# Second block's gate and value tiles 3 to 20 as seven half-depth, half-token block products for eight, with the weight sums on GpSimd and the gated tiles rounded later

## The chip, the cores and the metric

The kernel runs on one core of a Trainium2 chip. The metric is the device time of one execution in microseconds (us); lower is better. The core has a matrix engine, TensorE (PE in the rows; its weight loads are PEld), and three engines for elementwise work: VectorE (DVE), ScalarE (ACT) and GpSimd (POOL). SyncE (SP) issues the transfers from HBM. Each engine has a program of its own and goes through it in order; they are ordered among each other by semaphores only. Matmul results land in PSUM, everything else on the chip lies in SBUF. Both have 128 partitions.

## The reference

Two model blocks run one after the other on 512 tokens of width 1024, in float32. The change concerns the second block, which has two layers, and in it only the gated feed-forward network:

```python
def rmsnorm(x, g, eps=NORM_EPS):
    xf = x.astype(jnp.float32)
    y = xf * lax.rsqrt(jnp.mean(xf * xf, axis=-1, keepdims=True) + eps)
    return y.astype(x.dtype) * g

def swiglu(h, w_gate, w_up, w_down):
    return (jax.nn.silu(h @ w_gate) * (h @ w_up)) @ w_down

def second_block(x, ...):
    for l in range(DEPTH):
        x = x + 0.5 * swiglu(rmsnorm(x, ffn1_norm[l]), ffn1_w_gate[l], ffn1_w_up[l], ffn1_w_down[l])
        h = rmsnorm(x, mix_norm[l])
        ...
        x = x + 0.5 * swiglu(rmsnorm(x, ffn2_norm[l]), ffn2_w_gate[l], ffn2_w_up[l], ffn2_w_down[l])
    return rmsnorm(x, final_norm)
```

There are two layers (DEPTH is 2); the dots in the loop stand for three token mixers, whose output is added to x. The hidden width is 2752, 21 tiles of 128 and one of 64. So the feed-forward network runs four times; each run is called a part below.

## The kernel before

**Layout.** Activations lie with the feature on the partition and the 512 tokens along the row. A weight tile is 128 x 128, and a *unit* is a piece of weights that comes in one transfer: eight such tiles side by side, 128 x 1024 (all eight depth steps k of one gate or value tile), or 128 x 896 for seven tiles of the down projection. A part has 43 units of gate and value (gate tile 0, value tile 0, gate tile 1, ...; the last holds the 64 columns of both) and then 24 of the down projection, three for each of eight output tiles.

**Precision.** A float32 product is made of three matmuls of a reduced type (fp32r in the rows): each operand is split into a rounded part `hi` and a remainder `lo`, and the sum is hi x hi + hi x lo + lo x hi. So a unit of eight tiles is 24 matmuls of 512 columns, and a gate and value tile is 48. The split of a unit is ScalarE's rounding (`Stream.split_hi`, L682) and VectorE's subtraction of 1024 columns (`Stream.split_lo`, L690). SyncE loads units into four raw buffers (`one_raw`), the split ones lie in three places (`two_w_hi`, `two_w_lo`), and `Stream.multiply` (L705) waits for the split and signals `unit_done`, on which the rounding of the unit three further on waits.

**A part.** The RMS norm's gain goes onto x first (ScalarE L597, `two_x_hi`; the remainder VectorE L602); the norm's factor for each token (`m.rstd`, made while the first units are multiplied) is multiplied onto the results. For each tile t, VectorE scales the gate product out of PSUM into one of two `mid` rows (L1482), ScalarE applies Silu to it in place (L1258), VectorE multiplies it with the value product from PSUM (L1488, the gated product) and scales again (L1491), ScalarE rounds the result to `two_h_hi` (L1262), and VectorE makes the remainder `two_h_lo` (L1496). Splits of the units to come stand between these steps, at places written out by hand: one ahead of the gated product, one ahead of the remainder.

```python
for t in range(FT2):
...
    st.split_lo(dve, u + min(2 * t + 5, IN2 + 3))
...
    st.split_lo(dve, u + min(2 * t + 6, IN2 + 4))
...
```

TensorE uses PSUM banks 2 (t mod 3) and the next for tile t. After the 22 tiles comes the down projection with 128 x 512 hidden tiles as the moving operand: each of the eight output tiles takes three units, of eight, seven and seven hidden tiles (its three thirds). In the very last part the last output tile is made in two token halves of 256 columns (`last_tile`, L1085).

**Parts and stages.** The four parts lie in three stages (`chain_stage`); the first part starts directly behind the last norm of the first block (its first three gate and value tiles run beside the end of that norm), the other three behind the output projection of a mixer or behind the part before. GpSimd has nothing to do in them.

## Time and profile before

| what | value |
|---|---|
| time, median of 3 runs | 3702.64 us (3702.22 to 3707.24) |
| profiled execution, span from first to last instruction | 3696.9 us |
| TensorE busy | 3586.1 us, 97% |
| VectorE busy | 2026.3 us, 55% |
| ScalarE busy | 1432.0 us, 39% |
| GpSimd busy | 139.1 us, 4% |
| DMA | 82 GB/s on average |
| mean granted TensorE clock | 0.984 of full speed |
| part starts (first scaling, L1482) | 1476.7, 2223.6, 2576.3, 3346.2 us |

A busy share is the time in which an engine had an instruction under way, over the span. The profile lists no time of its own for the profiled execution beside its span; the median of the runs lies 5.7 us above that span. A row of the timeline gives the start, the duration, the engine, the line of the program, the operation, and the operands with their shapes and types; what stands in brackets is how long the engine had been idle before it and which work ended that wait.

### The profile page before, as it was taken

To read this page: it belongs to the slowest core of one execution; us is meant where nothing else is said; L and a number is where in the kernel's file an instruction comes from. 1 tells how busy PE (TensorE), PEld (TensorE's weight loads), DVE (VectorE), ACT (ScalarE), POOL (GpSimd) and SP (SyncE) were. 2 spreads that over 40 slices of the span, in tenths; PEclk is the share of its full clock that TensorE was granted. 3 is DMA by queue.
4 is the path that set the end of the run, shared out by engine and by line. 5 is a ranking of instruction groups with operands and counts; after the bars stand their busy time and mean duration, and the time that the engine had idled before them with its cause. 6 is when DMAs were issued, how large, how long until landed. Compare 5 with 4: busy or idle time off the path is not lost. (4 is left out here: it accounts for less than half of the span.)

```text
span 3696.9 us, 61545 instructions
## 1 busy us (share of the span) xinstructions
PE 3586.1 (97%) x26295; PEld 3100.4 (84%) x26295; DVE 2026.3 (55%) x3385; ACT 1432.0 (39%) x2297; POOL 139.1 (4%) x189
## 2 busy tenths in 40 slices
PE   8999999899999998999999999999999999999999
PEld 8999999788899998888877678888888877668887
DVE  7667653544476635543478564444444478565443
ACT  6844332544453324332243343223222244343232
POOL 0000000011000000000003100000000002100000
PEclk9999999999999998999999999999999999999999
DMA  3232223122212232333320023333333320013332
GB/s 136 80 98 84 91 91 92 64 76 76 69 64 92 91 94 76 99 96 98 111 69 3 24 80 97 97 94 101 97 97 94 110 80 2 24 64 99 97 95 80
DMA packets 87872, 303.21 MB, mean 82 GB/s; under 512 B 9632, under 2 KB 11808, under 8 KB 87344
## 3 DMA queue, kind: packets, MB, share of 16 engines
q1 hardware_dynamic: 87600, 299.28, 25.7%
q8 instruction: 208, 3.41, 0.4%
q14 instruction: 64, 0.52, 0.0%
HBM read 297.11 MB, written 2.13 MB: 81 GB/s over the span
## 5 line engine op out<-in xcount | busy, mean ns | idle before, releaser
L690 DVE TENSOR_TENSOR two_w_lo<-one_raw,two_w_hi 128x1024 fp32r<-128x1024 f32 (+1 forms) x334 | 400.5, 1199 | 754.7 <-ACT two_w_hi L682 752.6
L705 PE MATMUL psum<-two_x_hi,two_w_hi 128*128 128x512 f32 x1768 | 694.6, 393 | 1.2 <-DVE two_rows L1488 0.9
L705 PE MATMUL psum<-two_x_hi,two_w_lo 128*128 128x512 f32 x1768 | 688.4, 389 | 0.0
L705 PE MATMUL psum<-two_x_lo,two_w_hi 128*128 128x512 f32 x1768 | 687.9, 389 | 0.0
L682 ACT CAST two_w_hi<-one_raw 128x1024 fp32r<-128x1024 f32 (+1 forms) x334 | 342.0, 1025 | 823.6 <-PE psum L705 817.1
L705 PEld LDWEIGHTS psum<-two_x_hi,two_w_hi 128*128 128x128 f32 x1768 | 331.8, 188 | 88.8 <-issue 17.8
L2286 PE MATMUL psum<-one_x_hi,one_w_hi 128*128 128x264 f32 (+1 forms) x1376 | 391.6, 285 | 7.8 <-DVE one_x_lo L790 7.3
L705 PEld LDWEIGHTS psum<-two_x_hi,two_w_lo 128*128 128x128 f32 x1768 | 331.8, 188 | 69.8
L705 PEld LDWEIGHTS psum<-two_x_lo,two_w_hi 128*128 128x128 f32 x1768 | 331.9, 188 | 69.4 <-issue 1.4
L2286 PE MATMUL psum<-one_x_lo,one_w_hi 128*128 128x264 f32 (+1 forms) x1376 | 389.4, 283 | 0.0
L2286 PE MATMUL psum<-one_x_hi,one_w_lo 128*128 128x264 f32 (+1 forms) x1376 | 389.0, 283 | 0.0
L705 PE MATMUL psum<-two_h_hi,two_w_hi 128*128 128x512 f32 x794 | 308.9, 389 | 0.0
L705 PE MATMUL psum<-two_h_hi,two_w_lo 128*128 128x512 f32 x794 | 308.9, 389 | 0.0
L705 PE MATMUL psum<-two_h_lo,two_w_hi 128*128 128x512 f32 x763 | 296.8, 389 | 0.0
L2286 PEld LDWEIGHTS psum<-one_x_hi,one_w_hi 128*128 128x128 f32 x1376 | 259.4, 189 | 10.3 <-DVE one_x_lo L790 9.6
L2286 PEld LDWEIGHTS psum<-one_x_lo,one_w_hi 128*128 128x128 f32 x1376 | 259.8, 189 | 0.0
L2286 PEld LDWEIGHTS psum<-one_x_hi,one_w_lo 128*128 128x128 f32 x1376 | 259.5, 189 | 0.0
L690 DVE TENSOR_TENSOR one_w_lo<-one_raw,one_w_hi 128x1024 fp32r<-128x1024 f32 (+2 forms) x145 | 170.6, 1179 | 124.8 <-ACT one_w_hi L682 123.0
L2286 PE MATMUL psum<-one_h_hi,one_w_hi 128*128 128x264 f32 (+1 forms) x704 | 198.9, 283 | 2.4 <-ACT one_pads L2391 2.4
L2286 PE MATMUL psum<-one_h_lo,one_w_hi 128*128 128x264 f32 (+1 forms) x704 | 199.0, 283 | 0.0
L2286 PE MATMUL psum<-one_h_hi,one_w_lo 128*128 128x264 f32 (+1 forms) x704 | 198.6, 282 | 0.0
L682 ACT CAST one_w_hi<-one_raw 128x1024 fp32r<-128x1024 f32 (+2 forms) x145 | 146.8, 1015 | 112.4 <-PE psum L2286 108.5
(540 smaller groups left out, 6723.1 us busy)
## 6 DMA issues: line engine op xcount, KB each, us to landing
one_raw<-in_swi_in SPq DMA_DIRECT2D x172, 512.0 KB, 3.5
one_raw<-in_ffn_in SPq DMA_DIRECT2D x88, 512.0 KB, 3.6
one_raw<-in_swi_out SPq DMA_DIRECT2D x64, 448.0 KB, 3.2
one_raw<-in_mix_in SPq DMA_DIRECT2D x54, 512.0 KB, 3.5
one_raw<-in_attn_w SPq DMA_DIRECT2D x32, 512.0 KB, 3.8
one_raw<-in_swi_out SPq DMA_DIRECT2D x32, 512.0 KB, 3.5
one_raw<-in_ffn_out SPq DMA_DIRECT2D x32, 448.0 KB, 3.3
one_raw<-in_lru_w SPq DMA_DIRECT2D x24, 512.0 KB, 5.3
```

What stands on the lines that cost most here:

```text
L682: self.nc.scalar.copy(self.place(u)[0], self.m.raw[:, u % self.RAW, 0:self.cols(u)]).then_inc(self.s["w_hi"], 1)
L690: self.nc.vector.tensor_tensor(lo, self.m.raw[:, u % self.RAW, 0:self.cols(u)], hi.bitcast(FP32), ALU.subtract).then_inc(self.s["w_lo"], 1)
L705: last = self.nc.tensor.matmul(self.m.ps[:, bank, :], a[:, w], b[:, k0 + k, :], start=(start and k == 0 and q == 0), stop=(stop and k == n ...
L2286: ins = nc.tensor.matmul(m.ps[:, bank + h, skip:HALF], a[:, w], b[:, k0 + k, h * HALF + skip:(h + 1) * HALF], start=(start and q == 0), st ...
```

## The change

**The products.** Tile t of gate and value, for t from 3 to 20, is one 2 x 2 block product: the weights are cut by gate and value and by the upper and lower four of the eight depth steps, the inputs by depth in the same way and by the first and last 256 tokens. That takes eight block products; the changed kernel makes seven, of sums of blocks (Winograd's form of Strassen's method). Each product is four depth steps of three matmuls with 256 columns. The products share their partial results through PSUM: ScalarE copies three partial sums of 256 columns out of it for each tile (`take`), and VectorE adds them to other products (`join`). The other tiles (0 to 2 and the one of 64) and the down projection keep their form.

**The sums.** For each tile GpSimd makes three sums of 128 x 512 of the raw weights for the next tile (`sum_weights`) and one for this one (`sum_last`), and at the part's start four of 128 x 1024 of the inputs (`sum_inputs`), from copies of x that ScalarE scales with the gain (`gain`, eight). The splits of a tile are now A and B (1024 columns), C, D and E (512): A and E come from the raw weights, B, C and D from the sums. A raw buffer is free again when the splits and the sums have read it.

**The hidden tiles.** The memory of the sums of inputs (`mixed`, `mixed_raw`) is that of the hidden tiles from 6 on. So the gated tiles are kept raw in `h_raw` (in the place of `two_h_lo`), and only tiles 0 to 5 are rounded as they come; the rounding and the remainders of tiles 6 to 20 come at the part's end.

```diff
+class Seven:
+    FIRST, LAST, NOW = 3, 20, 6
+    HALF, DEEP = SEQ // 2, KT // 2
...
+        self.done = self.count("done", [x for t in steps for x in (
+            now(t, 1, 2) + now(t - 1, 3, 4) + now(t, 6, 7, 5))])
...
+    def multiply(self, pe, t, p, bank, start, stop):
+        name = {1: "A", 2: "A", 6: "B", 5: "B", 7: "C", 3: "D", 4: "E"}[p]
+        pe.wait_ge(self.s["c_lo"], self.splits[t, name])
+        hi, lo = self.place(p)
+        for k in range(self.DEEP):
+            w, (x_hi, x_lo) = slice(k * P, (k + 1) * P), self.block(p, k)
+            for q, (a, b) in enumerate(((hi, x_hi), (hi, x_lo), (lo, x_hi))):
+                last = self.nc.tensor.matmul(self.m.ps[:, bank, 0:self.HALF], a[:, w], b, start=(start and k == 0 and q == 0),
+                                             stop=(stop and k == self.DEEP - 1 and q == 2), skip_group_check=True)
+        last.then_inc(self.s["c_done"], 1)
...
+    def first_products(self, pe, t):
+        self.emptied(pe, t, "A")
+        self.multiply(pe, t, 1, self.bank(t, "A"), True, False)
+        self.emptied(pe, t, "B")
+        self.multiply(pe, t, 2, self.bank(t, "B"), True, True)
...
+    def sum_inputs(self, pool):
+        pool.wait_ge(self.s["taken"], self.takes["x", KT - 1])
...
+            self.nc.gpsimd.tensor_tensor(raw(i, 1), left, right, ALU.subtract).then_inc(self.s["w_sum"], 1)
+
+    def sum_weights(self, pool, t):
...
+        self.nc.gpsimd.tensor_tensor(w[1], self.raw(t, 1, 0), self.raw(t, 1, 1), ALU.add).then_inc(self.s["w_sum"], 1)
+        if t > self.FIRST:
+            pool.wait_ge(self.s["c_lo"], self.splits[t - 1, "D"])
+        pool.wait_ge(self.s["w_sum"], self.sums[t, 1])
+        self.nc.gpsimd.tensor_tensor(w[0], w[1], self.raw(t, 0, 0), ALU.subtract).then_inc(self.s["w_sum"], 1)
+        self.nc.gpsimd.tensor_tensor(w[2], self.raw(t, 0, 0), self.raw(t, 1, 0), ALU.subtract).then_inc(self.s["w_sum"], 1)
+
+    def sum_last(self, pool, t):
+        w = self.m.w_sums[:, 0, :]
+        pool.wait_ge(self.s["c_lo"], self.splits[t, "B"])
+        self.nc.gpsimd.tensor_tensor(w, self.raw(t, 0, 1), w, ALU.subtract).then_inc(self.s["w_sum"], 1)
...
+                    for t in seven.tiles:
+                        seven.first_products(pe, t)
+                        if t > seven.FIRST:
+                            seven.last_products(pe, t - 1)
+                        seven.middle_products(pe, t)
+                    pe.wait_ge(s["scaled"], part.h + seven.LAST)
+                    st.multiply(pe, part.u + 2 * REST, 2 * (REST % 3), m.xs, 0, True, True)
+                    seven.last_products(pe, seven.LAST)
```

TensorE makes products 1 and 2 of a tile first, then 3 and 4 of the tile before, then 6, 7 and 5.

**VectorE inside the tiles.** Before, one tile's rows are these (the letters after the line are the operation, then output and inputs by the names in SBUF, and the shape); a psum among the inputs is a read from PSUM:

```order
L1482 TENSOR_TENSOR two_rows<-psum,two_rows 128x512
L690 TENSOR_TENSOR two_w_lo<-one_raw,two_w_hi 128x1024
L1488 TENSOR_TENSOR two_rows<-psum,two_rows 128x512
L1491 TENSOR_TENSOR two_rows<-two_rows 128x512
L690 TENSOR_TENSOR two_w_lo<-one_raw,two_w_hi 128x1024
L1496 TENSOR_TENSOR two_h_lo<-two_rows,two_h_hi 128x512
```

In the changed program a tile from 8 on has these. L1000 is a split (by their order B, C, A of the next tile, D, E), L1018 a join, L1024 and L1028 the scalings of the gate's two token halves, L1035 the gated product, L1816 the scaling behind it:

```order
L1000 TENSOR_TENSOR two_w_lo<-two_w_sums,two_w_hi 128x1024
L1000 TENSOR_TENSOR two_w_lo<-two_w_sums,two_w_hi 128x512
L1018 TENSOR_TENSOR two_rows<-psum,two_rows 128x256
L1024 TENSOR_TENSOR two_rows<-two_rows 128x256
L1000 TENSOR_TENSOR two_w_lo<-one_raw,two_w_hi 128x1024
L1028 TENSOR_TENSOR two_rows<-psum,two_rows 128x256
L1000 TENSOR_TENSOR two_extra_lo<-two_w_sums,two_extra_hi 128x512
L1018 TENSOR_TENSOR two_h_raw<-psum,two_rows 128x256
L1035 TENSOR_TENSOR two_rows<-two_h_raw,two_rows 128x512
L1816 TENSOR_TENSOR two_h_raw<-two_rows 128x512
L1000 TENSOR_TENSOR two_w_lo<-one_raw,two_w_hi 128x512
L1018 TENSOR_TENSOR two_h_raw<-psum,two_rows 128x256
```

Six rows become twelve, the hidden tile's remainder has left, and the gated product reads both operands from SBUF.

**GpSimd.** Before, it has no row in a part. Now a part begins with the four sums of inputs, and then each tile has four sums of weights:

```order
L1044 TENSOR_TENSOR two_mixed_raw<-two_mixed_raw 128x1024 x4
L1050 TENSOR_TENSOR two_w_sums<-one_raw 128x512
L1054 TENSOR_TENSOR two_w_sums<-two_w_sums,one_raw 128x512
L1055 TENSOR_TENSOR two_w_sums<-one_raw 128x512
L1060 TENSOR_TENSOR two_w_sums<-one_raw,two_w_sums 128x512
```

All of these are new; the last one of a tile waits for VectorE's split B, the second for the split D of the tile before.

**The start of a part, ScalarE and VectorE.** On ScalarE, the rows behind the square root of the norm (L626) are before:

```order
L626 ACTIVATE two_rows<-psum,eps 128x512
L1258 ACT_TABLE_LOAD
L1258 ACTIVATE two_rows<-two_rows 128x512
L1262 CAST two_h_hi<-two_rows 128x512
L1258 ACTIVATE two_rows<-two_rows 128x512
L682 CAST two_w_hi<-one_raw 128x1024
```

In the first part they now are (L969 the copies of x, L1511 Silu, L1517 the rounding of a hidden tile, L975 the roundings of the sums of inputs, L995 those of the weights):

```order
L626 ACTIVATE two_rows<-psum,eps 128x512
L969 ACTIVATE two_mixed_raw<-x_tokens,vectors 128x2x256 x8
L1511 ACT_TABLE_LOAD
L1511 ACTIVATE two_rows<-two_rows 128x512
L1517 CAST two_h_hi<-two_h_raw 128x512
L975 CAST two_mixed<-two_mixed_raw 128x1024 x2
L1511 ACTIVATE two_rows<-two_rows 128x512
L975 CAST two_mixed<-two_mixed_raw 128x1024 x2
L1517 CAST two_h_hi<-two_h_raw 128x512
L995 CAST two_w_hi<-one_raw 128x1024
```

And VectorE, from the first scaling (L1801) to the split A of tile 3 (the first L1000), with the remainders of the sums of inputs in L980:

```order
L1801 TENSOR_TENSOR two_rows<-psum,two_rows 128x512
L1810 TENSOR_TENSOR two_rows<-psum,two_rows 128x512
L1816 TENSOR_TENSOR two_h_raw<-two_rows 128x512
L1822 TENSOR_TENSOR two_h_lo<-two_h_raw,two_h_hi 128x512
L1801 TENSOR_TENSOR two_rows<-psum,two_rows 128x512
L980 TENSOR_TENSOR two_mixed<-two_mixed_raw,two_mixed 128x1024 x2
L1810 TENSOR_TENSOR two_rows<-psum,two_rows 128x512
L1816 TENSOR_TENSOR two_h_raw<-two_rows 128x512
L1822 TENSOR_TENSOR two_h_lo<-two_h_raw,two_h_hi 128x512
L980 TENSOR_TENSOR two_mixed<-two_mixed_raw,two_mixed 128x1024 x2
L1801 TENSOR_TENSOR two_rows<-psum,two_rows 128x512
L1000 TENSOR_TENSOR two_w_lo<-one_raw,two_w_hi 128x1024
```

The eight copies stand between the norm's root and the first Silu; the four remainders of 1024 columns stand ahead of split A, for which product 1 of tile 3 waits. In the other parts the splits of units 4 to 6 (L703) stand between these rows as well.

**The end of a part, VectorE.** Behind the join of product 7 of tile 20 and the split of the down projection's first unit, VectorE has these rows up to the split (L703) for the down projection's second third. L1822 is the remainder of a hidden tile (x2: two of them), and the shapes with 64 are the last, narrow tile:

```order
L1822 TENSOR_TENSOR two_h_lo<-two_h_raw,two_h_hi 128x512 x2
L1028 TENSOR_TENSOR two_rows<-psum,two_rows 128x256
L1801 TENSOR_TENSOR two_rows<-psum,two_rows 64x512
L1822 TENSOR_TENSOR two_h_lo<-two_h_raw,two_h_hi 128x512 x2
L1018 TENSOR_TENSOR two_h_raw<-psum,two_rows 128x256
L1035 TENSOR_TENSOR two_rows<-two_h_raw,two_rows 128x512
L1816 TENSOR_TENSOR two_h_raw<-two_rows 128x512
L1822 TENSOR_TENSOR two_h_lo<-two_h_raw,two_h_hi 128x512 x2
L1810 TENSOR_TENSOR two_rows<-psum,two_rows 64x512
L1816 TENSOR_TENSOR two_rows<-two_rows 64x512
L1822 TENSOR_TENSOR two_h_lo<-two_h_raw,two_h_hi 128x512 x2
L703 TENSOR_TENSOR two_w_lo<-one_raw,two_w_hi 128x896
```

Before, each remainder stood inside its tile, and nothing but a split and the remainder of the last tile stood between the last scaling and the down projection.

## Rows read from the trace of the kernel before

**Rows 1.** The page, part 1: busy time, share of the span, instructions.

```profile
PE 3586.1 (97%) x26295; PEld 3100.4 (84%) x26295; DVE 2026.3 (55%) x3385; ACT 1432.0 (39%) x2297; POOL 139.1 (4%) x189
```

**Rows 2.** Windows, inside a part: length, busy PE, PEld, DVE, ACT, POOL, PEclk, DMA, GB/s.

```profile
1520.00:1640.00 120.00, 120.00 (x531) 99.34 (x531) 54.72 (x68) 35.73 (x44) 0.00 (x0) 1.00 0.31 97
```

**Rows 3.** Timeline of VectorE inside the gate and value tiles.

```profile
1568.08 1.23 DVE L690 TENSOR_TENSOR two_w_lo<-one_raw,two_w_hi 128x1024 fp32r<-128x1024 f32 x1 [3.01 <-ACT two_w_hi L682]
1569.22 0.68 DVE L1488 TENSOR_TENSOR two_rows<-psum,two_rows 128x512 f32<-128x512 f32 x1
1569.94 0.69 DVE L1491 TENSOR_TENSOR two_rows<-two_rows 128x512 f32<-128x512 f32 x1
1573.52 1.23 DVE L690 TENSOR_TENSOR two_w_lo<-one_raw,two_w_hi 128x1024 fp32r<-128x1024 f32 x1 [2.89 <-ACT two_w_hi L682]
1574.66 0.69 DVE L1496 TENSOR_TENSOR two_h_lo<-two_rows,two_h_hi 128x512 fp32r<-128x512 f32 x1
1575.26 0.69 DVE L1482 TENSOR_TENSOR two_rows<-psum,two_rows 128x512 f32<-128x512 f32 x1
1578.96 1.23 DVE L690 TENSOR_TENSOR two_w_lo<-one_raw,two_w_hi 128x1024 fp32r<-128x1024 f32 x1 [3.01 <-ACT two_w_hi L682]
```

**Rows 4.** The chain that ended last, in order of time: start, length, what.

```profile
3338.31 332.34 PE psum L705 x1466
3670.65 13.19 PE psum L1085 x110
```

**Rows 5.** Lines by form, VectorE, from the second block's token mixers.

```profile
L3539 DVE TENSOR_TENSOR two_ring<-psum,two_ring 128x256 f32<-128x256 f32 x8 | 3.2, 420 | 1.6 <-PE psum L3327 1.6
```

**Rows 6.** Lines by form, ScalarE: the gain onto x, and the Silu table.

```profile
L597 ACT ACTIVATE two_x_hi<-x_tokens,vectors 128x512 fp32r<-128x512 f32 x40 | 29.0, 725 | 152.7 <-DVE x_tokens L1404 152.7
...
L1258 ACT ACT_TABLE_LOAD x4 | 5.1, 1283 | 0.1
```

**Rows 7.** Lines by form, GpSimd, from the second block's token mixers.

```profile
L3517 POOL TENSOR_TENSOR two_y<-two_ring 128x512 f32<-128x512 f32 x6 | 7.6, 1268 | 0.5
L2685 POOL TENSOR_TENSOR two_low<-two_low,two_high 128x768 f32<-128x768 f32 x4 | 7.2, 1813 | 0.0
```

**Rows 8.** Timelines of GpSimd and VectorE in the first block's attention.

```profile
712.27 0.30 POOL L1867 COPY one_convs<-one_bias 128x128 f32<-128x128 f32 x1
712.31 1.32 DVE L2012 TENSOR_TENSOR one_w_lo<-one_raw,one_w_hi 128x1024 fp32r<-128x1024 f32 x1
...
719.06 1.33 DVE L2012 TENSOR_TENSOR one_w_lo<-one_raw,one_w_hi 128x1024 fp32r<-128x1024 f32 x1
719.26 1.19 POOL L1855 COPY one_convs<-one_bias 128x16 f32<-128x16 f32 x1
720.41 1.28 POOL L1856 TENSOR_TENSOR one_convs<-one_bias,causal 128x512 f32<-128x512 f32 x1
720.51 1.75 DVE L2055 TENSOR_SCALAR one_logits<-one_logits,stat 128x400 f32<-128x400 f32 x2
721.84 0.42 DVE L2055 TENSOR_SCALAR one_logits<-one_logits,stat 128x400 f32<-128x400 f32 x1
721.93 1.45 POOL L1856 TENSOR_TENSOR one_convs<-one_bias,causal 128x512 f32<-128x512 f32 x1
```

**Rows 9.** The page, part 6: issues of a unit's transfer, median from issue to landing.

```profile
one_raw<-in_swi_in SPq DMA_DIRECT2D x172, 512.0 KB, 3.5
```

**Rows 10.** Lines by form: the down projection's splits and matmuls.

```profile
L690 DVE TENSOR_TENSOR two_w_lo<-one_raw,two_w_hi 128x896 fp32r<-128x896 f32 x64 | 69.9, 1093 | 124.1 <-ACT two_w_hi L682 124.1
L705 PE MATMUL psum<-two_h_hi,two_w_hi 128*128 128x512 f32 x794 | 308.9, 389 | 0.0
```

**Rows 11.** Timelines at the starts of the third part and the first.

```profile
2562.59 0.39 PE L705 MATMUL psum<-two_x_hi,two_w_hi 128*128 128x512 f32 x1
2573.96 1.05 ACT L682 CAST two_w_hi<-one_raw 128x1024 fp32r<-128x1024 f32 x1 [4.85 <-PE psum L705]
2596.40 1.05 ACT L682 CAST two_w_hi<-one_raw 128x1024 fp32r<-128x1024 f32 x1 [1.27 <-PE psum L705]
...
1472.63 0.69 ACT L626 ACTIVATE two_rows<-psum,eps 128x512 f32<-128x512 f32 x1 [2.46 <-PE psum L621]
1478.94 0.50 PE L705 MATMUL psum<-two_x_hi,two_w_hi 128*128 128x512 f32 x1 [0.86 <-DVE two_rows L1488]
```

**Rows 12.** Timeline and window of TensorE behind a wait in the first block.

```profile
163.50 0.36 PE L268 MATMUL psum<-one_hid_hi,one_lru_mix_hi 128*128 128x264 f32 x1 [2.94 <-ACT one_lru_cross L356]
164.50:168.00 3.50, 3.50 (x18) 0.51 0.40 109
```

More of the change, by code:

```diff
@@ L1121, in _ @@
                         first_units(part, rms, (0, 1))
-                    for t in range(3 if carried and part.first else 1, FT2):
-                        if t >= 3:
-                            pe.wait_ge(s["product"], part.h + t - 2)
-                        for g in range(2 if t < REST else 1):
+                    seven = sevens[part]
+                    for t in range(3 if carried and part.first else 1, seven.FIRST):
+                        for g in range(2):
                             st.multiply(pe, part.u + 2 * t + g, 2 * (t % 3) + g, m.xs, 0, True, True)
+                    for t in seven.tiles:
[6 more added lines that the diff above has]
+                    seven.last_products(pe, seven.LAST)
                     pe.wait_ge(s["std_ready"], part.p + 1)
@@ L1253, in _, with open_gate @@
                 if part.kind == "ffn":
-                    st.split_hi(act, u + 4)
-                    for t in range(FT2):
+                    seven = sevens[part]
+                    def open_gate(t):
                         act.wait_ge(s["scaled"], part.h + t + 1)
@@ new lines, in _ @@
+                    seven.take(act, seven.LAST, "u4")
+                    st.split_hi(act, u + IN2 + 1)
+                    act.wait_ge(s["c_done"], seven.done[seven.LAST, 5])
+                    for t in range(seven.NOW, seven.NOW + 4):
+                        round_hidden(t)
+                    open_gate(seven.LAST)
+                    for t in range(seven.NOW + 4, seven.NOW + 6):
+                        round_hidden(t)
+                    open_gate(REST)
+                    for t in range(seven.NOW + 6, seven.NOW + 8):
+                        round_hidden(t)
@@ L1263, in _ @@
+                    st.split_hi(act, u + IN2 + 2)
+                    act.wait_ge(s["c_done"], seven.done[seven.LAST, 4])
+                    for t in range(seven.NOW + 8, seven.LAST - 2):
+                        round_hidden(t)
+                    st.split_hi(act, u + IN2 + 3)
+                    for t in range(seven.LAST - 2, FT2):
+                        round_hidden(t)
+                    st.split_hi(act, u + IN2 + 4)
                     u += IN2
@@ new lines, in _ @@
+                    for t in seven.tiles:
+                        if t > seven.FIRST:
+                            seven.join(dve, t - 1, "C22")
+                            seven.split_lo(dve, t, "B")
+                        seven.split_lo(dve, t, "C")
+                        dve.wait_ge(s["hidden"], part.h + t - 1)
+                        seven.join(dve, t, "C11")
+                        seven.scale_first(dve, t)
+                        if t < seven.LAST:
+                            seven.split_lo(dve, t + 1, "A")
+                        else:
+                            st.split_lo(dve, u + IN2)
+                        if t > seven.FIRST:
+                            seven.scale_last(dve, t - 1)
+                        seven.split_lo(dve, t, "D")
+                        if t > seven.FIRST:
+                            seven.join(dve, t - 1, "C21")
+                            seven.gated(dve, t - 1)
+                            to_hidden(t - 1)
+                        seven.split_lo(dve, t, "E")
+                        if t - 1 < seven.NOW:
+                            rest_of_hidden(t - 1)
@@ new lines, in _ @@
+                    seven.join(dve, seven.LAST, "C22")
+                    st.split_lo(dve, u + IN2 + 1)
+                    for t in range(seven.NOW, seven.NOW + 2):
+                        rest_of_hidden(t)
+                    seven.scale_last(dve, seven.LAST)
+                    scale(REST)
+                    rest_of_hidden(seven.NOW + 2)
+                    rest_of_hidden(seven.NOW + 3)
+                    seven.join(dve, seven.LAST, "C21")
+                    seven.gated(dve, seven.LAST)
@@ new lines, in _ @@
+                    to_hidden(seven.LAST)
+                    for t in range(seven.NOW + 4, seven.NOW + 6):
+                        rest_of_hidden(t)
+                    gated(REST)
+                    to_hidden(REST)
+                    for t in range(seven.NOW + 6, seven.NOW + 8):
+                        rest_of_hidden(t)
+                    st.split_lo(dve, u + IN2 + 2)
+                    for t in range(seven.NOW + 8, seven.LAST - 2):
+                        rest_of_hidden(t)
+                    st.split_lo(dve, u + IN2 + 3)
@@ L1498, in _ @@
+                    for t in range(seven.LAST - 2, FT2):
+                        rest_of_hidden(t)
+                    st.split_lo(dve, u + IN2 + 4)
                     u += IN2
```

320 lines of the change are left out of this document (278 added, 42 removed).

## The prediction, made before the changed kernel had run

> **What bounds the kernel now.** I read the page's busy line first: TensorE is busy for 97% of a span of 3696.9 us, VectorE for 55%, ScalarE for 39%, GpSimd for 4% [rows 1]. Then the busy time by window: in a stretch inside the gate and value tiles TensorE is busy all of the time, VectorE 46%, GpSimd not at all [rows 2]. The VectorE timeline gives the length of a tile there: a weight split stands at 1568.08 and the same one of the next tile at 1578.96, so a tile takes 10.88 us [rows 3]. It holds 48 matmuls of 512 columns; the chain of waits has 1466 of these in 332.34 us, 226.7 ns each, and 48 x 226.7 is 10.88 again [rows 4]. So these tiles are bound by TensorE alone, and what takes away matmul time there shortens the span as long as the engines that feed it keep up. The durations are those of the profiled execution, whose span lies 5.7 us under the median of 3702.64. I take these 5.7 us as lying around the span and unchanged: the profiled execution then stands for 3702.6, which to the tenth is the median of the runs, and the sum below goes from there.
>
> **What the change removes from TensorE.** Tiles 3 to 20 are 18 tiles in each of four parts, 72 in all. A tile becomes 7 products of 4 x 3 matmuls of 256 columns, 84. The rows have that very shape in the last output tile: 110 matmuls in 13.19 us, 119.9 ns [rows 4]. 84 x 119.9 is 10.07 us, not 7/8 of 10.88 (9.52), because a half-length matmul costs more than half. The gain is 0.81 us a tile, **-58.3 us** over 72, if nothing else waits.
>
> **What it puts on VectorE.** One tile's queue, by the rows of order above: two splits of 1024 columns (A, B), three of 512 (C, D, E), three joins, one first and one last scaling of 256, the gated product and its scaling of 512. A 1024 split lasts 1.23 us and the next instruction starts 0.09 before it ends, so it takes 1.14 of the queue; one of 512 lasts 0.68 to 0.69 and takes 0.60 [rows 3]. For 256 columns the nearest row is 0.42 [rows 5], 0.34 of the queue. Two (the first join, the gated product) have a successor that needs their result; I count these full. Sum: 2 x 1.14 + 4 x 0.60 + 4 x 0.34 + 0.42 + 0.69 = 7.15, say 7.2 us. That alone would fit in 10.07. ScalarE fits too: two copies of 1024 (1.05 each, [rows 11]) and seven shorter steps of at most 0.73 [rows 6] are 7.2.
>
> **What it puts on GpSimd, and whom that stops.** Four sums of 512 columns a tile; such a row takes 1.27 us [rows 7]. The rows show that GpSimd and VectorE stop each other. At 719.26 a GpSimd copy of 16 columns takes 1.19 us: it ends 0.06 after a VectorE subtraction with two SBUF inputs (719.06 to 720.39). The other way, a subtraction of the split's own shape begins at 712.31, with a GpSimd copy running to 712.57, and takes 1.32 in place of 1.23. Two scalings from 720.51, alongside GpSimd's sum (720.41 to 721.69), take 1.75 together, though the second, from 721.84, takes 0.42: the first ended at about 721.92, 0.23 after the sum. And the sum from 721.93 takes 1.45, to 1.12 after that second scaling [rows 8]. So whoever comes second waits for the whole of the other and then needs its streaming time only: about 0.54 us for 512 VectorE columns, 1.07 for 1024 (712.57 to 713.63), 1.11 for a GpSimd sum. Instructions with one operand in PSUM I take as not stopped; [rows 5] is one, some of them beside GpSimd's work. Of VectorE's twelve, eight have two SBUF inputs.
>
> The Trainium skill, SBUF — State Buffer, on the shared port pair, states the same exclusion, for VectorE with two SBUF inputs against a GpSimd instruction that reads SBUF, and says that it is held for the whole instruction. By that last point the eight instructions and the four sums would stand end to end, 11.4 us a tile; by the rows the loser's start-up overlaps the wait, and the tile is the 10.4 laid out next.
>
> I lay one tile out with B at 0. B ends 1.23; C follows and ends 1.83; the last sum of this tile (it waits for B) gets the port at C's end, to 2.95. The first join is not stopped; the first scaling is, to 3.23 (0.6 late). The next tile's first sum needs a weight unit whose buffer the previous E has freed at -0.25, and 3.5 us from issue to landing [rows 9] puts it at 3.4; A, ready at 3.25, comes ahead of it and ends 4.36. That sum then holds the port to 5.5, and D ends 6.0 (0.7 late). After D the next sum runs 6.1 to 7.4; the gated product is pushed to 7.9 (0.9), the last sum runs behind it to 9.0, and the scaling behind that to 9.56 (0.9). E and the join end 10.5, and the next B starts at 10.42. 7.2 + 3.2 of waits is 10.4: VectorE, not TensorE, sets the tile. (If the landing came 0.2 us sooner the sum would go ahead of A and the tile be 10.75; if each sum fell beside a PSUM instruction, 10.07 from TensorE.) I take 10.42: it loses 0.35 of the 0.81 in 16 tiles a part, 5.6 us. In tiles 4 to 6 a rounding remainder (0.60) is still in the queue: 1.8. Together 7.4 a part, **+29.6 us**.
>
> **The end of a part.** The remainders of tiles 6 to 20 now come after the tiles. Behind product 3 of tile 20 VectorE has, ahead of the fifteenth remainder that the second third of the down projection waits for: a scaling of 256, one of 512, seven remainders, a join, two gated products with their scalings, a split of 896 (1.09 [rows 10]): 9.2 us. TensorE has product 4 (1.44) and the first third, 24 x 0.2267 = 5.44: 6.9. It waits 2.3, and in front of the last third (seven remainders and a split, 5.2, against 21 x 0.2267 = 4.76) 0.5. 2.8 x 4, **+11.2 us**. Before, the down projection's matmuls waited for nothing [rows 10].
>
> **The start of a part.** This is where most is queued. ScalarE makes eight scaled copies of x first, 0.63 each by the nearest row (0.73, and I take 0.10 off, as for VectorE's neighbours) [rows 6], 5 us, and the Silu table (1.28) loads behind them. In the third part, from its first matmul at 2562.59 [rows 11], the rounding of unit 3 ends 12.4 in; copies to 17.4, table to 18.7, first Silu 19.3, rounding of unit 4 at 20.2. GpSimd then makes four sums of 1024 columns; rows of 512 and 768 take 1.27 and 1.81 [rows 7], so about 2.35 each, and three of 512. From 20.2 VectorE has ahead of A of tile 3: two splits, two gated products and their scalings, two remainders, two scalings, four remainders of 1024 columns and A itself, 13.7 us, and stands 0.7 for ScalarE. By the same laying out the sums stop it for 1.8, 1.5, 2.1, 1.1, 0.6 and 1.1: A ends at about 42.0. TensorE had units 0 to 5 done at 33.8 (2596.40, where the rounding that waits for unit 5's place begins); with 0.9 of waits for units 4 and 5 that is 34.7, so it stands 7.3 us more. 8.2 x 3 = 24.6. In the first part the first six units are done at 1478.1; there the copies run from 1473.3 to 1478.4 [rows 11] and the same queue (its splits already made) puts A at 1500. That is 22 us, of which 0.9 was idle before. The loss is 21. Together **+45.6 us**. If no sum stopped VectorE, A would come at 34.7 and 1496.7: 1 and 17.
>
> **The clock.** Behind a wait of 2.9 us that ended at 163.5 the granted clock was 0.51, the 1.2 GHz level, for 3.5 us [rows 12], which costs 1.7. I take 2 us for each of the four starts, **+8 us**, and nothing for the ends, whose waits are shorter.
>
> **Nothing for**: the loads (the same units, 3.5 us each in 10.4), the renamed waits, the removed signals.
>
> Sum: -58.3 + 29.6 + 11.2 + 45.6 + 8 = +36.1, 3702.6 + 36.1 = **3739 us**, 1.0% slower.
>
> **Rivals.**
> 1. *GpSimd's sums cost VectorE nothing* (faster). For it: only copies, not sums, are seen stopping a two-input subtraction; the long stops by a sum are of a one-input scaling. Against it: both fit one port. Then -58.3 + 11.2 + 17 + 3 + 4 for the clock = -23: 3680. It decides at the stretch of tiles 8 to 19: at 10.1 us a tile this is the case. Chance 0.17.
> 2. *The port is held for whole instructions* (slower still): then the eight two-input instructions (2 x 1.23 + 5 x 0.69 + 0.42 = 6.33) and the sums (4 x 1.27) stand end to end, 11.4 a tile, 64 x 0.98 = 63 more: 3802. For it: nothing runs beside the holder in [rows 8]. Against it: the first scaling ended 0.23 after the sum, not 0.42. Chance 0.10. (The page named above would have it so.)
> 3. *The exclusion holds in the tiles, but the starts cost a quarter*, because ScalarE runs ahead or the sums fall where VectorE waits anyway: -34 and -6 of clock, 3699, the same. For it: VectorE is idle half of the plain tiles; against it: A stands behind all of it in program order. Chance 0.13.
>
> My forecast has 0.52; 0.08 lies between it and rival 3. The median of before can be told from a change within about 0.2% (7 us). Faster: rival 1 and a little of rival 3, 0.20; the same 0.13; slower 0.67. The forecast's own range is 3715 to 3765; for 8 in 10 I reach to rival 1 and most of the way to rival 2: 3678 to 3790.
>
> **What would show it.** Tiles 8 to 19: spacing of the 256-column last scaling, 10.4 (10.1 for rival 1, 11.4 for rival 2), with the 512 scaling behind the gated product lasting about 1.5 and the GpSimd sums 1.3 to 2. Start: TensorE idle some 20 us in the first part and 7 in the others ahead of the first 256-column matmul. End: 2 to 3 us idle in front of the second third. 256-column matmuls at 120 ns. I am wrong if VectorE's two-input instructions keep 0.69 and 1.23 beside the sums, or if the first tile of a part starts without a wait.

## The result, and the profile after

The changed kernel takes 3775.8 us (median of 4 runs, 3772.5 to 3777.6), the kernel before on the same chip 3704.7 (3702.2 to 3707.2): a ratio of 1.0191, 95% interval 1.0177 to 1.0205, 71 us more. The forecast was 36 us slower, so the direction was right and the size was half of what came.

The page's busy line answers to [rows 1]:

```profile
PE 3567.3 (95%) x28887; PEld 3195.3 (85%) x28887; DVE 2514.4 (67%) x3905; ACT 1650.8 (44%) x2777; POOL 657.5 (17%) x493
```

TensorE's busy time fell by 18.8 us only, and it is now idle for 207 us of a span of 3774.4, where it was idle for 111 of 3696.9. The window inside the tiles (length, busy PE, PEld, DVE, ACT, POOL, PEclk, DMA, GB/s) answers to [rows 2]:

```profile
1580.00:1700.00 120.00, 117.71 (x946) 114.96 (x946) 117.28 (x138) 61.96 (x105) 69.56 (x42) 1.00 0.33 106
```

VectorE, 46% busy there before, is at 98%. Its timeline, from a split B to the next, is the answer to [rows 3]; "x2" is B and C together:

```profile
1603.39 1.81 DVE L1000 TENSOR_TENSOR two_w_lo<-two_w_sums,two_w_hi 128x1024 fp32r<-128x1024 f32 x2
1605.12 0.41 DVE L1018 TENSOR_TENSOR two_rows<-psum,two_rows 128x256 f32<-128x256 f32 x1
1605.57 1.06 DVE L1024 TENSOR_TENSOR two_rows<-two_rows 128x256 f32<-128x256 f32 x1
1606.55 1.21 DVE L1000 TENSOR_TENSOR two_w_lo<-one_raw,two_w_hi 128x1024 fp32r<-128x1024 f32 x1
1607.69 0.41 DVE L1028 TENSOR_TENSOR two_rows<-psum,two_rows 128x256 f32<-128x256 f32 x1
1608.03 1.45 DVE L1000 TENSOR_TENSOR two_extra_lo<-two_w_sums,two_extra_hi 128x512 fp32r<-128x512 f32 x1
1609.39 0.41 DVE L1018 TENSOR_TENSOR two_h_raw<-psum,two_rows 128x256 f32<-128x256 f32 x1
1609.84 1.54 DVE L1035 TENSOR_TENSOR two_rows<-two_h_raw,two_rows 128x512 f32<-128x512 f32 x1
1611.41 1.67 DVE L1816 TENSOR_TENSOR two_h_raw<-two_rows 128x512 f32<-128x512 f32 x1
1613.01 0.68 DVE L1000 TENSOR_TENSOR two_w_lo<-one_raw,two_w_hi 128x512 fp32r<-128x512 f32 x1
1613.61 0.41 DVE L1018 TENSOR_TENSOR two_h_raw<-psum,two_rows 128x256 f32<-128x256 f32 x1
1613.94 1.81 DVE L1000 TENSOR_TENSOR two_w_lo<-two_w_sums,two_w_hi 128x1024 fp32r<-128x1024 f32 x2
```

and GpSimd's in the same stretch:

```profile
1604.68 1.67 POOL L1060 TENSOR_TENSOR two_w_sums<-one_raw,two_w_sums 128x512 f32<-128x512 f32 x1 [2.70 <-DVE two_w_lo L1000]
1606.97 1.95 POOL L1050 TENSOR_TENSOR two_w_sums<-one_raw 128x512 f32<-128x512 f32 x1 [0.62 <-DMA one_raw<-in_swi_in]
1609.55 1.28 POOL L1054 TENSOR_TENSOR two_w_sums<-two_w_sums,one_raw 128x512 f32<-128x512 f32 x1 [0.63 <-DVE two_extra_lo L1000]
1610.79 1.74 POOL L1055 TENSOR_TENSOR two_w_sums<-one_raw 128x512 f32<-128x512 f32 x1
```

Read the two against each other. The four VectorE rows of 1.06, 1.45, 1.54 and 1.67 us are those that read two operands from SBUF while a sum runs; alone they take 0.42 to 0.69. Each ends 0.28 (256 columns) or 0.55 us (512) after the sum beside it: L1035 at 1611.38, the sum L1054 at 1610.83. A GpSimd sum that comes second waits as well: L1050 starts at 1606.97, split A ends at 1607.76, and the sum ends 1.16 behind that. The rows with a PSUM operand take 0.41 wherever they fall: L1028 lies wholly inside L1050, and over the whole run the 118 rows of L1018 and L1028 that lie inside a GpSimd row take 0.41 to 0.42. The spacing of a tile is 1613.94 - 1603.39, 10.55; over the whole stretch it is 10.56 (10.42 forecast, TensorE's own 10.08).

The waits of TensorE (engine and line, for whom; us in all, times, the longest) came, before, to 0.9 us for the gated product at the first part's start [rows 11] and nearly nothing else inside the parts; now these rows stand in the list:

```profile
PE psum L929 <- DVE two_w_lo L1000: 43.8, 4, 22.1
PE psum L929 <- ACT two_rows L1010: 33.4, 64, 1.6
...
PE psum L718 <- DVE two_h_lo L1822: 11.6, 4, 2.9
```

The first is the four starts of parts, 22.1 and three of 7.2 (forecast 22 and 7.3): in the third part VectorE's split A ends at 2651.24,

```profile
2650.02 1.22 DVE L1000 TENSOR_TENSOR two_w_lo<-one_raw,two_w_hi 128x1024 fp32r<-128x1024 f32 x1
```

and TensorE's product 1 begins behind it, 7.24 us late:

```profile
2651.38 0.55 PE L929 MATMUL psum<-two_x_hi,two_w_hi 128*128 128x256 f32 x1 [7.24 <-DVE two_w_lo L1000]
```

The second is the tiles, where ScalarE's copies out of PSUM stand behind VectorE. The third is the four ends, 2.9 each, all ahead of the down projection's second third; 2.3 was forecast there, and 0.5 ahead of the last third, where no wait came.

The granted clock behind these waits (windows: length, PE busy, PEclk, DMA share, GB/s), first at the second part's start, then at the first part's end:

```profile
2284.60:2289.60 5.00, 4.72 (x22) 0.50 0.13 30
2290.00:2295.00 5.00, 5.00 (x44) 1.00 0.16 56
1712.70:1716.10 3.40, 3.38 (x9) 0.57 0.47 135
```

At the 1.2 GHz level 22 matmuls took the time of 44. TensorE worked 19.7 us at that level behind the four starts, and 3.4, 3.4 and 6.2, 13.0 in all, behind three of the four ends.

### The profile page after: what moved, and what is told of

It is laid out like the page before. It is cut to its first block and busy times, and to the rows that moved or that the text cites. A ratio compares the mean times of both kernels' runs of the same rounds, so it can differ in the third digit from the quotient of the medians.

```text
span 3774.4 us, 69338 instructions
## 1 busy us (share of the span) xinstructions
PE 3567.3 (95%) x28887; PEld 3195.3 (85%) x28887; DVE 2514.4 (67%) x3905; ACT 1650.8 (44%) x2777; POOL 657.5 (17%) x493
## 5 line engine op out<-in xcount | busy, mean ns | idle before, releaser
L929 PE MATMUL psum<-two_mixed,two_w_hi 128*128 128x256 f32 x2304 | 426.9, 286 | 33.4 <-ACT two_rows L1010 33.4
L703 DVE TENSOR_TENSOR two_w_lo<-one_raw,two_w_hi 128x1024 fp32r<-128x1024 f32 (+1 forms) x190 | 235.7, 1242 | 300.6 <-ACT two_w_hi L695 298.4
L929 PEld LDWEIGHTS psum<-two_mixed,two_w_hi 128*128 128x128 f32 x2304 | 358.5, 192 | 46.3 <-ACT two_rows L1010 46.3
L695 ACT CAST two_w_hi<-one_raw 128x1024 fp32r<-128x1024 f32 (+1 forms) x190 | 191.1, 1009 | 385.2 <-PE psum L718 378.9
L929 PE MATMUL psum<-two_mixed,two_w_lo 128*128 128x256 f32 x1152 | 326.1, 283 | 0.0
L718 PE MATMUL psum<-two_h_hi,two_w_hi 128*128 128x512 f32 x794 | 312.5, 394 | 11.8 <-DVE two_h_lo L1822 11.6
L703 DVE TENSOR_TENSOR one_w_lo<-one_raw,one_w_hi 128x1024 fp32r<-128x1024 f32 (+2 forms) x145 | 170.7, 1179 | 124.8 <-ACT one_w_hi L695 123.0
L718 PE MATMUL psum<-two_x_hi,two_w_hi 128*128 128x512 f32 x616 | 247.3, 402 | 2.7 <-DVE two_w_lo L703 2.7
L718 PE MATMUL psum<-two_x_hi,two_w_lo 128*128 128x512 f32 x616 | 240.6, 391 | 0.0
L718 PE MATMUL psum<-two_x_lo,two_w_hi 128*128 128x512 f32 x616 | 240.2, 390 | 0.0
L929 PEld LDWEIGHTS psum<-two_mixed,two_w_lo 128*128 128x128 f32 x1152 | 220.9, 192 | 0.0
L929 PE MATMUL psum<-two_x_hi,two_w_hi 128*128 128x256 f32 x576 | 167.8, 291 | 43.8 <-DVE two_w_lo L1000 43.8
```

The costliest lines, as they stand in the source:

```text
L695: self.nc.scalar.copy(self.place(u)[0], self.m.raw[:, u % self.RAW, 0:self.cols(u)]).then_inc(self.s["w_hi"], 1)
L703: self.nc.vector.tensor_tensor(lo, self.m.raw[:, u % self.RAW, 0:self.cols(u)], hi.bitcast(FP32), ALU.subtract).then_inc(self.s["w_lo"], 1)
L718: last = self.nc.tensor.matmul(self.m.ps[:, bank, :], a[:, w], b[:, k0 + k, :], start=(start and k == 0 and q == 0), stop=(stop and k == n ...
L929: last = self.nc.tensor.matmul(self.m.ps[:, bank, 0:self.HALF], a[:, w], b, start=(start and k == 0 and q == 0), stop=(stop and k == self. ...
```

## The experiments

Theory: GpSimd's sums stop VectorE's instructions that have two SBUF inputs, so VectorE sets the tile and the starts; VectorE's queue also sets the ends. Rivals: ScalarE's copies, the order of the waits, or memory traffic in general sets them, whoever makes the sums.

**1. The sums left out.**

```diff
-                "C": lambda: self.m.w_sums[:, 2, :], "D": lambda: self.m.w_sums[:, 0, :], "E": lambda: self.raw(t, 1, 1)}[name]()
+                "C": lambda: self.raw(t, 0, 0), "D": lambda: self.raw(t, 0, 1), "E": lambda: self.raw(t, 1, 1)}[name]()
...
-                seven.sum_inputs(pool)
-                seven.sum_weights(pool, seven.FIRST)
...
```

> GpSimd's sums are left out, of weights and inputs; the splits read the raw weights and the scaled copies instead, so the output is not the reference's, while every other instruction keeps its shape and place. Theory (the sums stop VectorE at a shared SBUF port): VectorE's two-input instructions are back at 0.42, 0.69 and 1.23 us, a steady tile falls from 10.56 to 10.07 (TensorE's 84 matmuls), tiles 4 to 6 from 11.9 to about 10.1, TensorE's wait at the start of parts 2 to 4 from 7.2 to about 1 and in the first part from 22 to about 17; the time falls by about 75 us to near 3700. Rival (VectorE's queue, ScalarE's copies or the order of the waits set the tile, whoever makes the sums): the tile stays above 10.4 and the time above 3750.

3681.6 us, ratio to before 0.9944 (0.9929 to 0.9959). VectorE's rows at the same place of a tile:

```profile
1601.40 0.69 DVE L1029 TENSOR_TENSOR two_rows<-two_h_raw,two_rows 128x512 f32<-128x512 f32 x1
1602.13 0.69 DVE L1803 TENSOR_TENSOR two_h_raw<-two_rows 128x512 f32<-128x512 f32 x1
1602.74 0.69 DVE L994 TENSOR_TENSOR two_w_lo<-one_raw,two_w_hi 128x512 fp32r<-128x512 f32 x1
1605.46 0.42 DVE L1012 TENSOR_TENSOR two_h_raw<-psum,two_rows 128x256 f32<-128x256 f32 x1 [2.04 <-ACT two_rows L1004]
```

and TensorE's waits:

```profile
PE psum L927 <- DVE two_w_lo L994: 16.4, 4, 14.7
PE psum L716 <- DVE two_h_lo L1809: 11.6, 4, 2.9
```

The 1.54 and 1.67 are 0.69 again, VectorE has 2 us to spare, the spacing is 10.08, and the starts are 14.7 and three of 0.6. The ends are untouched. The time is 18 us under the 3700 that this run's expectation named: the starts fell further than it said, and the half-clock stretches behind three of them, which it had not counted, went too. This is the first rival of the prediction, which gave 3680.

**2. The sums of weights on VectorE.**

```diff
-        self.nc.gpsimd.tensor_tensor(w[1], self.raw(t, 1, 0), self.raw(t, 1, 1), ALU.add).then_inc(self.s["w_sum"], 1)
...
+            self.nc.vector.tensor_tensor(out, left, right, op).then_inc(self.s["w_made"], 1)
```

> The four sums of weights of each tile move from GpSimd to VectorE (the sums of inputs stay on GpSimd); the result is the reference's. Theory (a sum on GpSimd costs VectorE more in waiting, 3.26 us a tile, than the four sums would take on VectorE, 4 x 0.60 = 2.4): VectorE's tile is 7.3 + 2.4 + some 0.2 = 9.9, under TensorE's 10.07, which is the spacing; tiles 4 to 6 at about 10.6; the starts about as before. About 40 us less: 3736. Rival (VectorE's long instructions have another cause, such as ScalarE's or the DMAs' traffic): VectorE's tile is 10.56 + 2.4 = 13 us and the time rises by over 150 us.

3749.0 us, 1.0126 (1.0111 to 1.0141): 27 us less than the changed kernel by the medians, 24 by the ratios, with the work moved onto the engine that was full. The rival's 13 us a tile is out. But 40 less were expected: the spacing was 10.48, not 10.07, and VectorE waited in each tile:

```profile
1605.22 0.42 DVE L1018 TENSOR_TENSOR two_h_raw<-psum,two_rows 128x256 f32<-128x256 f32 x1 [0.24 <-ACT two_rows L1010]
1606.10 1.82 DVE L1000 TENSOR_TENSOR two_w_lo<-two_w_sums,two_w_hi 128x1024 fp32r<-128x1024 f32 x2 [0.45 <-ACT two_w_hi L995]
```

An engine that waits 0.7 us a tile isn't the bound. Experiments 3 and 4 look for what is.

**3. The same, with ScalarE's copy of product 6 ahead of Silu.**

```diff
                         if t > seven.FIRST:
+                            seven.take(act, t, "u2")
                             open_gate(t - 1)
                         seven.split_hi(act, t, "E")
-                        seven.take(act, t, "u2")
```

> As the run with the weight sums on VectorE, and on ScalarE the copy of product 6's sum (take u2) stands ahead of Silu and split E. There the tile was 10.48 us with VectorE idle for 0.7 of it, so its queue was not full. Theory (a ring of waits through four engines sets 10.48: the last scaling on VectorE, Silu and split E on ScalarE, then take u2, product 5, take u4, the rounding of B, and VectorE's B to scaling again): with take u2 out of the ring the tile is TensorE's 10.07 to 10.1, about 28 us less than that run: near 3720. Rival (VectorE's queue of 9.8 us busy with its waits is the bound): the spacing stays at 10.4 to 10.5, the time near 3749.

3755.7 us, 1.0144 (1.0125 to 1.0164), spacing 10.43. That is the spacing that the rival named, so this run by itself decides nothing between the two; experiment 4 does. My theory of the ring missed a link. The copy now waited itself:

```profile
1602.51 0.37 ACT L1010 COPY two_rows<-psum 128x256 f32<-128x256 f32 x1 [3.33 <-DVE two_h_raw L1018]
```

It waits for VectorE's join of product 4 of the tile before, which reads the half row that this copy writes, and that join stood behind two sums, the last scaling and split D.

**4. The sums on VectorE, with that join and the last scaling early.**

```diff
                             seven.split_lo(dve, t + 1, "A")
-                            seven.sum_weights(dve, t + 1, (1, 3))
...
                             seven.scale_last(dve, t - 1)
+                            seven.join(dve, t - 1, "C21")
+                        if t < seven.LAST:
+                            seven.sum_weights(dve, t + 1, (1, 3))
                         seven.split_lo(dve, t, "D")
```

> As the first run with the weight sums on VectorE (ScalarE's order as in the changed kernel); on VectorE the last scaling and the join of product 4 of the tile before now stand directly behind split A, ahead of two of the sums and split D. Moving take u2 alone left 10.43 us: there ScalarE's take u2 waited 3.3 us for that join, whose operand lies where take u2 writes. Theory (the ring runs through VectorE's place for that scaling and join): both come 1.5 us or more earlier, take u2 finds product 6 done, and the tile is TensorE's 10.07 to 10.1; 13 to 16 tiles a part at 0.4 less, some 22 us less than that run: near 3727. Rival (16 instructions on VectorE with their dependencies need 10.4 in whatever order): 10.4 again, near 3749.

3729.3 us, 1.0073 (1.0060 to 1.0086), as expected, so VectorE's sixteen instructions do fit. The spacing of the last scaling is TensorE's:

```profile
1619.67 0.42 DVE L1028 TENSOR_TENSOR two_rows<-psum,two_rows 128x256 f32<-128x256 f32 x1
...
1629.75 0.42 DVE L1028 TENSOR_TENSOR two_rows<-psum,two_rows 128x256 f32<-128x256 f32 x1
```

VectorE does twelve instructions and four sums in 10.08 us without GpSimd, and twelve alone in 10.56 with it.

**5. The seven products from tile 5 on.**

```diff
-    FIRST, LAST, NOW = 3, 20, 6
+    FIRST, LAST, NOW = 5, 20, 6
```

> Seven products from tile 5 on instead of 3, tiles 3 and 4 plain; all else as in the changed kernel. Theory (the starts wait because VectorE's queue ahead of split A is longer than the plain tiles' matmul time; 21.8 us more of plain matmuls cover it): no wait at the start of parts 2 to 4 (7.2 + 0.9 before), at most some 2 us in the first part (22 before), and no half-clock stretch there; eight tiles go back to 10.88 (+3). In all about 50 us less: 3725. Rival (VectorE's queue is the bound from the part's start on, so more plain tiles only move the wait to a later place): waits of 4 us or more stay in each part, the time above 3750.

3722.7 us, 1.0057 (1.0042 to 1.0072). No wait for split A is left:

```profile
PE psum L929 <- ACT two_rows L1010: 21.5, 54, 1.6
PE psum L718 <- DVE two_h_lo L1824: 11.6, 4, 2.9
PE psum L718 <- DVE two_w_lo L703: 7.8, 7, 5.1
...
PE psum L718 <- DVE two_rows L1812: 2.9, 1, 2.9
```

In parts 2 to 4 two waits of 0.4 and 0.5 us for plain units are left of the start. In the first part 8 us of the 22 came back (5.1 and 2.9, at most 2 were expected), in front of plain units: ScalarE's eight copies stand ahead of their roundings, a place that I had not counted.

**6. The end of a part reordered.**

```diff
-                    for t in range(seven.NOW, seven.NOW + 2):
+                    for t in range(seven.NOW, seven.NOW + 7):
                         rest_of_hidden(t)
                     seven.scale_last(dve, seven.LAST)
```

> At the end of a part seven remainders of hidden tiles instead of two are placed ahead of the last scaling of tile 20, where VectorE stood idle for 3.1 us, and ScalarE's roundings with them. Theory (TensorE's 2.9 us ahead of the second third is VectorE's queue there): the wait falls under 0.6 us and the half-clock stretch behind it goes with it: 4 x (2.3 + up to 1.7), 10 to 16 us less, about 3762. Rival (the remainders are only late elsewhere): the same wait stands ahead of the last third, and the time stays within 4 us.

3757.0 us, 1.0151 (1.0134 to 1.0168; the changed kernel has 1.0191). VectorE fills with remainders the 3.1 us in which it had waited for product 3:

```profile
1694.88 4.29 DVE L1819 TENSOR_TENSOR two_h_lo<-two_h_raw,two_h_hi 128x512 fp32r<-128x512 f32 x7
1699.29 0.42 DVE L1028 TENSOR_TENSOR two_rows<-psum,two_rows 128x256 f32<-128x256 f32 x1
```

The row of 11.6 us for the remainders is gone from the waits, and no stretch at half clock is left in the down projections (118.6 us each for 122.4 to 123.7, the last part's 120.0 for 122.8).

**7. No rounding inside the seven-product tiles.**

```diff
-    FIRST, LAST, NOW = 3, 20, 6
+    FIRST, LAST, NOW = 3, 20, 3
```

> The changed kernel with the hidden tiles 3 to 5, too, rounded at the part's end (NOW 3 for 6). Theory (tiles 4 to 6 take 11.94 us for 10.56 because a remainder stands in VectorE's queue and pushes split A beside a GpSimd sum): all tiles from 4 on take 10.56, which saves 3.4 us a part; three more remainders stand at the part's end, and the wait ahead of the second third grows from 2.9 to about 4.7. Net about 6 us less: 3770. Rival (the first tiles are slow because VectorE has to catch up after the start, whatever stands in them): they stay near 11.9 and the end costs more: 3783.

3762.8 us, 1.0161 (1.0140 to 1.0181), 13 less by the medians and 11 by the ratios, where 6 were expected. Tile 4 takes 9.78 and tiles 5 to 19 take 10.56, so the first tiles aren't slow by themselves. The place that I named for the longer end was wrong: the wait is 3.7 to 3.8 us ahead of the down projection's first third, not the second.

```profile
PE psum L718 <- DVE two_h_lo L1822: 11.5, 3, 3.8
...
PE psum L718 <- issue: 3.7, 1, 3.7
```

**8 to 11. Combined kernels.** All four have the seven products from tile 5, the weight sums on VectorE and the end order (of experiment 6). The first three have the copies of x behind the first hidden tile:

```diff
-                    seven.gain(act)
                     for t in range(seven.FIRST):
...
+                        if t == 0:
+                            seven.gain(act)
```

The first two also have ScalarE's order of experiment 3, with NOW 6 and 5.

> Seven products from tile 5 on, weight sums on VectorE, take u2 ahead of Silu, the end order, and at a part's start ScalarE's eight copies of x behind the first hidden tile. If each cause is as found, 64 tiles at 10.07 to 10.1 for 10.88 (51 us), no wait ahead of the seven products and at a part's end, some 1 us a part for the tiles that still hold a remainder and some 2 for clock and fill: about 3656, 1.2% faster than before. If the causes only hide one another, a wait comes back in the start or in the tiles and the time stays above 3690.

> As the other combined kernel with hidden tile 5 left to the end too (NOW 5). If a remainder in a seven-product tile costs more than at the end: 1 to 3 us less than the other; if VectorE's slack in the tiles (10.07 less about 9.8) takes it, the same within 1 us or 1 to 2 us more.

3703.0 us, 1.0000 (0.9988 to 1.0011), and 3698.4, 0.9994 (0.9983 to 1.0005). The first missed its 3656 by 47 us: with the order of experiment 3 the ring is closed, and the spacing is 10.43 here, too. The second lies 4.6 us under it by the medians and 2 by the ratios; the intervals overlap, so what NOW 5 is worth isn't shown. The next has VectorE's order of experiment 4, ScalarE's old one and NOW 5; the last also makes the copies of x on GpSimd:

```diff
-            self.nc.scalar.activation(self.m.mixed_raw[:, at:at + 2, 0, (k - k0) * self.HALF:(k - k0 + 1) * self.HALF],
+            self.nc.gpsimd.tensor_scalar(self.m.mixed_raw[:, at:at + 2, 0, (k - k0) * self.HALF:(k - k0 + 1) * self.HALF],
```

> The combined kernel with NOW 5 (tiles at 10.43), with the last scaling and the join of product 4 early on VectorE and ScalarE's old order. Theory: tiles at 10.07 to 10.1, about 0.35 x 14 x 4 = 20 us less than that kernel: 3679, faster than before by 0.6%. Rival (another ring closes at 10.3 or more): above 3690.

> As the kernel beside it, with the eight scaled copies of x made by GpSimd, ahead of its four sums of inputs, so that ScalarE's queue at a part's start holds only the two roundings more. Theory (the 6.8 and 3.6 us that the first part still stands, and 1.9 in the others, are ScalarE's copies ahead of the splits of units 6 and 7, and the sums behind them): the 6.8 goes, 0.9 is left of it, the 3.6 at most stays; 6 to 12 us less than the kernel beside it. Rival (GpSimd's copies stop VectorE and end later than ScalarE's did): the wait ahead of product 6 grows by what the other gives, and the time is the same or above.

3677.8 us, 0.9931 (0.9914 to 0.9947), and 3672.1, 0.9917 (0.9904 to 0.9930): both faster than the kernel before, by 24 and 30 us. The first is what was expected. The 6 us between the two aren't shown by their times, whose intervals overlap. In the last the window inside the tiles is

```profile
1580.00:1680.00 100.00, 100.00 (x814) 99.04 (x814) 94.59 (x156) 54.59 (x93) 0.00 (x0) 1.00 0.34 110
```

TensorE without a gap, VectorE at 95%. With the copies off ScalarE, the wait of 6.8 us for a plain unit, which the first part of the kernel beside it has, is 0.4. What is left of the start is one wait in the first part, for split A, which stands behind the remainders of the sums of inputs. These sums end at 1499.1 here, since the copies took GpSimd 13.6 us, and at 1493.1 in the kernel beside it, where the wait is 3.7; the rival had that much right:

```profile
PE psum L929 <- DVE two_w_lo L1001: 9.8, 1, 9.8
```

## Why the prediction went wrong in its size

From the first product of a part to its first matmul of the down projection the changed kernel takes 201.4 us in the second part (2284.9 to 2486.3; the four lie between 200.8 and 202.4, 201.5 on average). Without the sums that is 187.0 in three parts (2253.5 to 2440.5 in the second). Plain tiles would take 18 x 10.88 + 24 x 0.2267 = 201.3. With that, term by term:

| step | forecast | measured, and from what |
|---|---|---|
| fewer, shorter matmuls | -58.3 | 4 x (187.0 - 201.3) = -57.2 |
| VectorE stopped in the tiles | +29.6 | 4 x (201.5 - 187.0) = 58.0, less 9.9 of clock: +48 |
| ends of parts | +11.2 | 4 x 2.9 = +11.6 |
| starts of parts | +45.6 | 22.1 - 0.9 and 3 x (7.2 + 0.9) = +45.5 |
| clock | +8 | half of 19.7 and of 13.0: +16.4 |
| sum | +36.1 | +64.3; by the medians +71 |

**What was right.** Products, starts and ends agree within about 1 us. For the ends that is partly luck: 0.6 more came ahead of the second third, and the 0.5 ahead of the last third didn't come. For the starts the path was right too: in the third part A ends 42.3 us behind the first matmul, where the forecast said 42.0. (Its terms give that, 20.2 + 13.7 + 8.2 = 42.1, only if the 0.7 for ScalarE is within the 13.7.) The exclusion was right in its form: the loser needs its streaming time behind the winner, 0.55 us for 512 VectorE columns where 0.54 was forecast and 1.16 for a sum where 1.11 was. Experiments 1, 2 and 4 show that it comes with GpSimd's sums. The Trainium skill, SBUF — State Buffer, Who interferes with whom, says that a VectorE instruction with two SBUF inputs contends with a GpSimd one that reads SBUF, and one with at most one SBUF input, outside certain faster modes, doesn't: the rows agree (1.54 us for 0.69, and 0.41 inside L1050). The Trainium skill, SBUF — State Buffer, Terms, also says that the loser is fully blocked while the other holds the port, for the full instruction: that holds for the wait. The instruction then needs 0.55 us for the 0.69 that it takes alone, so its start-up runs meanwhile, and the tile was 10.56 and not the 11.4 of the second rival.

**The step that was mis-sized most** is "I take 10.42 ... In tiles 4 to 6 a rounding remainder (0.60) is still in the queue: 1.8. Together 7.4 a part": it measured 12. The spacings against TensorE's 10.08 say where: tiles 4 to 6 lose 1.86 each, tile 7 gives back 0.31, tiles 8 to 19 lose 0.48 each and tile 20 loses 0.70, 11.7 in all. Two things in it. The steady tile is 10.56: the join ahead of the gated product has a successor that needs its result, too (0.45 for 0.34, most of the difference), which I had not counted; 0.14 x 16 is 2.2 a part. And in tiles 4 to 6, 11.94 us each, the remainder costs more than its 0.60, because it pushes everything behind it: the sum L1050 then meets split A instead of D, and a split of 1024 columns waits.

```profile
2323.57 2.31 DVE L1000 TENSOR_TENSOR two_w_lo<-one_raw,two_w_hi 128x1024 fp32r<-128x1024 f32 x1
```

```profile
2323.31 1.49 POOL L1050 TENSOR_TENSOR two_w_sums<-one_raw 128x512 f32<-128x512 f32 x1
```

The sum won by 0.26 us, and A took 2.31 for 1.21. Beyond the steady tile and the 0.60 that is 3 x 0.78 - 0.8 (the tile behind them takes 9.77) = 1.5 a part; experiment 7 shows tiles 4 to 6 at 9.78, 10.56 and 10.56 without the remainder. The other 0.6 is a seventeenth tile, which I had left out, and tile 20's 10.78. I had laid out one steady tile and added to it, where the next step would have been to lay out the tile with the remainder as well.

**The clock** was the other: "nothing for the ends, whose waits are shorter". They are as long as the wait of [rows 12] from which I priced the starts (2.9 us), and three of them had a stretch at half clock behind them, 6.5 us where nothing was forecast; the starts came to 9.9 for 8. Experiment 6 took the waits away, and those stretches with them.

**What stays open** are the last 7 us; the interval of the ratio puts the 71 between 66 and 76. A run lies 1.8 us above its span (3776.2 for 3774.4), not 5.7 as I took it. By that the profile of before stands for a run of about 3698.7, and the two profiles differ by 77 us. Of these, 10 us lie outside the four parts, in code that the change doesn't touch: 2.6 before the first, 4.6 and 2.8 in the two mixers. A part of that is the granted clock, which is low at other places in one profile than in the other. This stretch in the first block, for example (before, then after), has half the clock in the second:

```profile
50.90:54.30 3.40, 3.40 (x30) 1.00 0.02 5
50.90:54.30 3.40, 3.40 (x18) 0.50 0.00 0
```

Ahead of the first part TensorE works 50.1 us at the low level after and 45.6 before; half of the difference is 2.3 of the 2.6 us. In the first mixer it is 27.3 for 20.5, which is 3.4 of the 4.6. In the second it is 27.3 for 30.5, so the 2.8 there have another cause, which I don't know. The kernels of this study give 411 to 417 us for the first mixer, and before has 411.3.

## What to carry to other kernels

Work that an idle engine takes over isn't free when its instructions stop those of the busy one: here four sums cost VectorE 3.25 us of waiting a tile, and about 2.4 (4 x 0.60) when it made them itself. Lay out the tile with the extra instruction as well as the steady one, since an exclusion is priced by who meets whom. And where the fullest engine has small waits in every tile, look for a ring through several engines, and for the operand in it that shares a place with another, before counting busy time.

## What was not expected of the hardware

The low level of TensorE's clock came behind waits as short as 2.9 us, at three of four such ends, and cost some 1.7 us there for each 3.4 at that level, more than half of the wait itself.

In some parts one tile took 12.2 to 12.3 us for 10.56, at a place that changes from kernel to kernel (at most one a part, and only with the sums on GpSimd). TensorE stands 1.2 to 1.3 us there, and the tile behind gives back 0.8. The rows lead to one copy on ScalarE, which begins 0.28 us later than in the tiles beside it (1.01 idle for 0.73):

```profile
3550.16 0.37 ACT L1010 COPY two_rows<-psum 128x256 f32<-128x256 f32 x1 [1.01 <-DVE two_h_raw L1018]
3551.09 1.77 DVE L1000 TENSOR_TENSOR two_w_lo<-two_w_sums,two_w_hi 128x512 fp32r<-128x512 f32 x1 [0.16 <-ACT two_w_hi L995]
```

The rounding of C stands behind that copy, so split C comes when the sum L1060 already runs, and takes 1.77 for 0.68. The sums behind it then meet other instructions than usual; in this tile L1050 wins against split A, which takes 2.32, as in tiles 4 to 6. A quarter of a microsecond on an engine that is half idle so costs the tile 1.8 us, 1.0 with what the next one gives back. Why the copy begins late no row tells.
